# Query, key and value projections of a latent attention as split products instead of plain f32 products

## The reference

```python
def mla_branch(c_q, c_kv, k_r, cos, sin, q_norm_g, kv_norm_g, w_uq, w_uk, w_uv):
    B, S, _ = c_q.shape
    q = (rmsnorm(c_q, q_norm_g) @ w_uq).reshape(B, S, MLA_HEADS, MLA_QK)
    q_nope = q[..., :MLA_NOPE]
    q_rope = apply_rope(q[..., MLA_NOPE:], cos[:, :, None, :], sin[:, :, None, :])
    k_rope = apply_rope(k_r, cos, sin)
    ckv = rmsnorm(c_kv, kv_norm_g)
    k_nope = (ckv @ w_uk).reshape(B, S, MLA_HEADS, MLA_NOPE)
    v = (ckv @ w_uv).reshape(B, S, MLA_HEADS, MLA_V)
    return causal_mla_attention(q_nope, q_rope, k_nope, k_rope, v)
```

## Time and profile before

| | |
|---|---|
| median of 3 runs | 2916.43 us (2915.56 to 2927.52) |
| the profiled execution's own time | 2920.05 us |
| its span, first to last instruction | 2918.3 us |
| TensorE (PE) busy | 2780.2 us, 95% of the span |
| ScalarE (ACT) busy | 1304.3 us, 45% |
| VectorE (DVE) busy | 842.2 us, 29% |
| GpSimd (POOL) busy | 2069.2 us, 71% |
| mean granted TensorE clock | 0.977 of full speed |

### The profile page before, as it was taken

One profiled execution on the slowest core, in us unless ns is written; L12 is line 12 of the kernel. 1 busy time (PEld: TensorE's weight loads), 2 busy tenths in 40 slices (PEclk: granted clock), 3 DMA queues, 4 the chain that ended last, 5 costly groups with the idle time before them and its releaser, 6 DMA issues. The chain is left out here.

```text
span 2918.3 us, 46932 instructions
## 1 busy us (share of the span) xinstructions
PE 2780.2 (95%) x19086; PEld 2555.2 (88%) x19086; DVE 842.2 (29%) x1449; ACT 1304.3 (45%) x1882; POOL 2069.2 (71%) x919
## 2 busy tenths in 40 slices
PE   7999899999999998989999999899999999989998
PEld 6899799899899888879899898787989989978798
DVE  2552343112233153211211313432131132243212
ACT  4455444444444444344444444444444444454443
POOL 7788455888887934778798764267879877425786
PEclk9999999999999999989999998999999999899999
DMA  6556433555665532565565553245556555423554
GB/s 225 166 195 204 150 109 113 191 188 181 203 192 181 195 123 94 154 180 187 172 211 185 173 185 127 66 141 187 186 165 213 187 173 182 129 73 127 191 188 144
DMA packets 131325, 484.13 MB, mean 166 GB/s; under 512 B 14720, under 2 KB 14720, under 8 KB 130112
## 3 DMA queue, kind: packets, MB, share of 16 engines
q1 hardware_dynamic: 127296, 463.53, 48.9%
q0 software_dynamic: 3840, 17.81, 2.1%
HBM read 478.65 MB, written 2.62 MB: 165 GB/s over the span
## 5 line engine op out<-in xcount | busy, mean ns | idle before, releaser
L972 POOL TENSOR_TENSOR rest<-ring,upper 128x1024 fp32r<-128x1024 f32 (+2 forms) x848 | 2029.5, 2411 | 789.5 <-ACT upper L1723 768.1
L1723 ACT ACTIVATE upper<-ring 128x1024 fp32r<-128x1024 f32 (+2 forms) x848 | 884.6, 1052 | 889.7 <-DMA ring<-in_weights 888.9
L348 PE MATMUL psA<-xT_upper,upper 128*128 128x256 f32 x2944 | 411.1, 282 | 2.3 <-ACT arena L1723 2.3
L348 PE MATMUL psA<-xT_rest,upper 128*128 128x256 f32 x2944 | 413.1, 283 | 0.0
L348 PE MATMUL psA<-xT_upper,rest 128*128 128x256 f32 x2944 | 405.5, 280 | 0.0
L348 PEld LDWEIGHTS psA<-xT_upper,upper 128*128 128x128 f32 x2944 | 384.3, 189 | 16.2 <-ACT arena L1723 3.6
L348 PEld LDWEIGHTS psA<-xT_rest,upper 128*128 128x128 f32 x2944 | 379.7, 192 | 0.0
L348 PEld LDWEIGHTS psA<-xT_upper,rest 128*128 128x128 f32 x2944 | 372.8, 189 | 0.0
L1207 DVE TENSOR_TENSOR psA<-sil,psA 128x256 f32<-128x256 f32 x144 | 61.8, 429 | 951.3 <-ACT sil L1723 951.2
L348 PE MATMUL psY<-upper,hT_upper 128*128 128x512 f32 x704 | 205.5, 397 | 9.4 <-ACT upper L1723 5.8
L348 PE MATMUL psY<-upper,hT_rest 128*128 128x512 f32 x704 | 206.2, 398 | 0.0
(11 more groups left out here) (245 smaller groups left out, 3220.9 us busy)
## 6 DMA issues: line engine op xcount, KB each, us to landing
ring<-in_weights SPq DMA_DIRECT2D x880, 512.0 KB, 3.4
G<-in_rows POOLq DMA_DIRECT2D x6, 1024.0 KB, 7.0
G<-in_rows POOLq DMA_DIRECT2D x7, 512.0 KB, 6.9
arena<-rel_by_distance POOLq DMA_DIRECT2D x8, 256.0 KB, 18.2
x<-in_x SPq DMA_DIRECT2D x2, 512.0 KB, 5.7
par<-in_params POOLq DMA_DIRECT2D x4, 256.0 KB, 6.1
xn<-in_mem POOLq DMA_DIRECT2D x1, 1024.0 KB, 10.6
memory_transposed<-arena POOLq DMA_DIRECT2D x1, 1024.0 KB, 6.4
```

The source lines that it names most:

```text
L348: i = pe.matmul(out, lhsT, rhs, start=start, stop=stop)
L972: pool.tensor_tensor(rest[:, r, 0:n], ring[:, r, 0:n], upper[:, r, 0:n], ALU.subtract)\
L1723: act.activation(out, in_, func, **kw).then_inc(*up)
```

## The change

The six pieces get widths (768 for the four query pieces, 1024 for keys and values), so that ScalarE and GpSimd split them. The latents `cT` are split as well: ScalarE copies `cT` to `latents[0]` and VectorE writes `latents[1]`, each in two halves of 128 tokens (128x640). The three projections become three passes. ScalarE's order gets two more `upto`: pieces 111 and 112 ahead of the copy of the sums, 113 ahead of the copies of the keys. The two new tiles lie in a part of the memory overlay that is free at that time.

```diff
-WIDTHS = [_FFN + [PIECE] * 8 + [640] * 8 + [PIECE] * 26 + [0] * 6 + [PIECE] * 40 + _FFN,
+WIDTHS = [_FFN + [PIECE] * 8 + [640] * 8 + [PIECE] * 26 + [768] * 4 + [PIECE] * 42 + _FFN,
...
+        latents = tuple(nc.alloc_sbuf_tensor_at(n, [P, 5, S], F32R, offset=overlay + 4 * (12 + 5 * i) * S)
+                        for i, n in enumerate(("latent_upper", "latent_rest")))
...
@@ tensor, block1
+                for t in range(TT):
+                    pe.wait_ge(*sig["latent rests"].after(t))
                 for n in range(4):
-                    s, = shaped(piece(), 3 * 256, "p (k c) -> p k c", k=3)
-                    features(("uq", n), 2, lambda k: cT[:, k, :], 3, lambda n, k: s[:, k, n * P:(n + 1) * P])
+                    s = shaped(piece(), 3 * 256, "p (k c) -> p k c", k=3)
+                    lab = (("uq", n), 0)
+                    out = fill(pe, next_a(), lab)
+                    for j in range(2):
+                        for w, v, first, last in passes():
+                            for k in range(3):
+                                end = last and k == 2
+                                mm(out[:, j * S:(j + 1) * S], s[w][:, k, j * P:(j + 1) * P], latents[v][:, k], first and k == 0, end,
+                                   filled(lab) if end and j == 1 else None)
                     free()
...
-                    for k in range(2):
-                        mm(out, cT[:, 3 + k, t * P:(t + 1) * P], s[:, k, :], k == 0, k == 1,
-                           filled(("uv", t)) if k == 1 else None)
+                    for w, v, first, last in passes():
+                        for k in range(2):
+                            end = last and k == 1
+                            mm(out, latents[v][:, 3 + k, t * P:(t + 1) * P], s[w][:, k, :], first and k == 0, end,
+                               filled(("uv", t)) if end else None)
...
@@ vector, block1, behind line 1471
+                for t in range(TT):
+                    dve.wait_ge(*sig["latent uppers"].after(t))
+                    v = (ALL, ALL, slice(t * P, (t + 1) * P))
+                    tt_(latents[1][v], cT[v], latents[0][v], ALU.subtract).then_inc(*sig["latent rests"].up(t))
                 dve.wait_ge(*sig["forget log"].after(0))
...
@@ scalar, block1
                     copy(("hgate", t), GH[:, t, :], func=ACT.Silu, piece=103)
+                for t in range(TT):
+                    for h in range(2):
+                        act.wait_ge(*taken(("cT", t, h)))
+                    v = (ALL, ALL, slice(t * P, (t + 1) * P))
+                    go(latents[0][v], cT[v], ACT.Copy, sig["latent uppers"].up(t))
                 act.wait_ge(*sig["forget read"].after(1))
...
                 gate_out([2, 3])
+                upto(FFN_PIECES + 46)
                 for b in range(TT):
                     act.wait_ge(*taken(("c", b)))
                 act.wait_ge(*sig["sums made"].after(0))
                 go(GP, GC, ACT.Copy, sig["sums copied"].up(0))
+                upto(FFN_PIECES + 47)
                 for n in range(4):
                     copy(("uk", n), KT[0:64, 2 * n:2 * n + 2, :])
```

More of the change, by code:

```diff
@@ L727, in block1 @@
                     pe.wait_ge(*taken(("cT", 1, h)))
+                for t in range(TT):
+                    pe.wait_ge(*sig["latent rests"].after(t))
                 for n in range(4):
-                    s, = shaped(piece(), 3 * 256, "p (k c) -> p k c", k=3)
-                    features(("uq", n), 2, lambda k: cT[:, k, :], 3, lambda n, k: s[:, k, n * P:(n + 1) * P])
-                    free()
-                s, = shaped(piece(), PIECE, "p (k c) -> p k c", k=2)
-                features("uk", 8, lambda k: cT[:, 3 + k, :], 2, lambda n, k: s[:, k, n * 64:(n + 1) * 64], m=64)
+                    s = shaped(piece(), 3 * 256, "p (k c) -> p k c", k=3)
[7 more added lines that the diff above has]
+                                   filled(lab) if end and j == 1 else None)
+                    free()
@@ new lines, in block1 @@
+                s = shaped(piece(), PIECE, "p (k c) -> p k c", k=2)
+                for n in range(4):
+                    lab = ("uk", n)
+                    out = fill(pe, next_a(), lab)
+                    for j in range(2):
+                        c = (2 * n + j) * 64
+                        for w, v, first, last in passes():
+                            for k in range(2):
+                                end = last and k == 1
+                                mm(out[0:64, j * S:(j + 1) * S], s[w][:, k, c:c + 64], latents[v][:, 3 + k], first and k == 0, end,
+                                   filled(lab) if end and j == 1 else None)
```

## The result

The changed kernel takes 2932.26 us in the median of 20 runs, the kernel before 2919.57 us in the median of its 20. The ratio is 1.0044, 95% interval 1.0033 to 1.0056: 12.8 us slower, between 9.6 and 16.3. The forecast was 2936 us in a range of 2918 to 2942, with 0.54 on slower by over 0.5% and 0.44 on no such difference. The time lies in the range and the direction is right. The size falls just under the 0.5% bound, so that of the two cases it was the second, given the smaller chance, that came true.

A forecast was written before the change was run, and what follows sets the result against it. TensorE's work and the ScalarE-VectorE chain ending in L1492 bound the stage. 11.75 us late less 3.1 saved gives 8.6 per layer, 17.2 for two, plus 2.7 for the clock: 2936 us on the median's base, range 2918 to 2942.

The forecast's parts named there:

- TensorE's work: Behind the stall in the edited stage, split products take 12.81 us instead of 15.93, 3.1 us less per layer.
- ScalarE's chain: Two latent copies ahead of the first Exp make its table load and what follows 2.6 us late.
- Piece 107's margin: The last gate piece's rest is ready at 332.7, TensorE wants it at 333.28: 0.6 us of margin left.
- Piece 108's split ahead of L1477: GpSimd's split of the first query piece goes ahead of VectorE's L1477, adding 1.8 us; the gap comes 4.4 us late.
- No upper part of 109: ScalarE splits the second query piece only after the second Ln, done at 343.5; TensorE stalls 6.4 us.
- The scans wait for one split each: VectorE's four scans each wait for one GpSimd split, the last ending at 353.9; TensorE goes on 11.75 us late.
- rival B: The scans do not wait for GpSimd and end at 346.45; +1.1 us per layer, 2918.6 in all; chance 0.22.
- Rival C: VectorE keeps the port through its four scans after one split; +2.9 us per layer, 2925 in all; chance 0.15.
- The clock: TensorE's half clock behind long stalls costs layer 0 2.7 us, layer 1 has it already; +2.7 us in all.

The follow-up runs named there:

- latents_later: The changed kernel with ScalarE's latent copies moved behind its first gate copy and VectorE's subtractions behind the gap; ratio 1.0043 to the kernel before.
- uppers_early: The changed kernel with ScalarE splitting pieces 109 and 110 behind the first Ln, 111 and 112 ahead of the second Exp; ratio 1.0037 to the kernel before.
- splits_after_sums: The changed kernel with GpSimd waiting for the end of the scans before splitting piece 109; ratio 1.0025 to the kernel before.
- kv_reads_first: The kernel before with only keys and values split, two query banks read before the scans, copies, subtractions and piece 112's split placed in pauses or behind scans; 2907.19 us.

## Why the prediction was right

By its own steps, with times counted from the stage's start:

- **TensorE's work.** Behind the second stall, on full clock: the keys, 354.29 to 359.97, take 5.68 us for 48 products (predicted 5.73, so 64-column weights cost what was estimated), the values 2.79 us (2.78). Right.
- **ScalarE's chain.** The first table load 2.7 us late (2.6). latents_later puts it back and takes 2.6 us off the stage of layer 0. Right, and shown.
- **Piece 107's margin.** No wait between 317.17 and 328.66. Right.
- **Piece 108's split ahead of L1477.** 2.74 us for that operation, 1.5 us more than 1.22, where 1.8 was taken. Right.
- **No upper part of 109.** TensorE starts the second query piece 20.7 us into the stage (337.83 - 317.17), predicted 20.8 (343.5 - 322.73), after a stall of 6.10 us, predicted 6.4. Right. That this stall by itself is not the loss is what uppers_early adds.
- **The scans wait for one split each.** 9.20 us against a predicted 9.9 and against 2.44 for rival B. splits_after_sums shows the cause. That they are 0.7 us shorter than predicted is mostly a slip in the sum: it let the first split start with the first scan, though the split was ready earlier, and in the trace it did start 0.48 us earlier (337.86 against 338.34). TensorE resumes 31.2 us into the stage instead of 20.3, so 11.0 us late (11.75). Rival C, a port kept through all four scans, is out by the narrow windows.
- **The clock.** The step was a term of +2.7 us net. From the second stall's end to the diagonal products take 14.35 us in layer 0 and 15.01 in layer 1, against 12.81 at full clock: 1.5 and 2.2 us lost; before, layer 1 lost 2.7 us. Net +1.0. The direction was right; the size was too large by 1.7 us. The half clock began earlier, on piece 109 (0.81 us for three products ahead of the second stall, 340.84 - 340.03, against 0.36 at full clock), where the second stall hides it, as predicted. It is part of why that stall is 5.45 us and not the predicted 7.5.

The sum by the traces is 9.4 + 7.4 = 16.8 us, where the prediction had 19.9: 1.5 us less from the scans' end, 1.7 from the clock. The timed runs give 12.8 us, with 16.3 as the interval's end. So 0.5 us at least, and some 4 at the centre, stand between the traces' stages and the timed runs. Two things can be in it, and neither is settled: the half clock behind the old stall in layer 1 differs between traces (38.9 and 37.9 us), and the unedited parts of the program differ between executions by 5 to 10 us each. That the forecast of 2936 lies only 4 us above the measured 2932.26 is in part luck: it was built on a median of three runs, 2916.43, which 20 runs put at 2919.57, and on that base the same sum gives 2939.5. What held is the mechanism; the change itself, 19.9 us by the sum, was measured as 12.8.

So the change does on TensorE what it says, 3.1 us per layer less work behind the second stall, but lets TensorE go on 11.0 us later than before, for VectorE's sake. Five of the six new splits of a layer (one beside L1503, four beside the scans) fall into the one stretch where VectorE's operations with two SBUF inputs are what the whole stage waits for, and these operations didn't get through side by side with a split.

## What to carry to other kernels

Before work goes to an idle engine, look at what it shares, not only at how idle it is: GpSimd was idle here for 31.6 us, and five of its six new splits still cost the critical chain a wait each. Place such work in the pauses of the other engine's critical chain, or behind it (splits_after_sums and kv_reads_first each did this with one wait). And look first at the stall that is there already: two reads moved ahead took 3.7 us off the stage of layer 0, the split keys and values 2.2.

## What the runs showed of the hardware

The four scans (128x256, both inputs in SBUF) go from 0.67 us each to 2.2 to 2.8 us each when GpSimd has splits queued, and the two engines take turns here, one instruction each, also where VectorE's operations don't wait for one another. The Trainium skill's page "SBUF — State Buffer", section "Who interferes with whom", says that a VectorE instruction with two SBUF inputs contends with a GpSimd instruction that reads SBUF. This case's traces agree, and show it for the scan too (2.26 us for one that takes 0.67 alone). A small operation pays as much as a large one: two subtractions on 256 columns took 3.70 us beside two splits and 0.76 us without, so 1.5 us more each, as much as L1503 on 1024 columns (2.74 against 1.22). The turns are not a rule without exception: in the trace of before one operation on 4 columns (L1406, 166.06 us, 7.67 us long) lasted through three whole splits in a row, and no run here shows why.
